# Three page buffers for the sample attention, a seventh expert loaded ahead, and prompt scores in row halves

## What is computed

```
q, k, v, xl, gl = split(x @ w_in)                      # 1024 -> 5 x 512
prompt: s[m] = q[m] k[m]^T / 8, causal, per head, m in (0, 1), 64 wide each
        w = softmax(s[0]) - lam * softmax(s[1]);  o = w v
sample: the same, against 1024 cached keys/values and the 8 new ones
o  = rmsnorm(o) * g;   y = RG-LRU(xl) * gelu(gl)       # recurrence over the tokens
x1 = LN1(alpha * x + [o ; y] @ w_out)                  # 1024 x 1024
group = top-1 of 4, experts = top-2 of the 8 in it     # 32 experts
f  = sum of the two: (silu(x1 wg) * (x1 wu)) wd * weight   # 1024 -> 256 -> 1024
out = LN2(alpha * x1 + f)
```

## Time and profile before

| | |
|---|---|
| time before, median of 3 runs (lowest, highest) | 731.29 us (728.52, 731.52) |
| the profiled execution: its own time | 730.15 us |
| its span, first to last instruction | 728.5 us |
| PE busy | 630.7 us, 87% of the span |
| DVE, ACT, POOL busy | 267.3, 159.0, 111.2 us |
| moved by DMA | 184.46 MB, mean 253 GB/s |
| mean granted TensorE clock (1 is 2.4 GHz) | 0.959 |

### The profile page before, as it was taken

How to read it: one execution, slowest core, us unless ns; L and a number is a source line. 1 busy time by engine, 2 the same in 40 slices (tenths; PEclk the granted TensorE clock), 3 DMA queues, 4 the chain that set the end, 5 groups by cost and what they waited for, 6 DMA issues and landing times.

```text
span 728.5 us, 11355 instructions
## 1 busy us (share of the span) xinstructions
PE 630.7 (87%) x3948; PEld 405.0 (56%) x3948; DVE 267.3 (37%) x566; ACT 159.0 (22%) x322; POOL 111.2 (15%) x191
## 2 busy tenths in 40 slices
PE   6999999999995898979999879899887877777764
PEld 5777676467664565655454636656554444444321
DVE  1562269036456453543544671101110011000257
ACT  2001542143344442431000101111111111111122
POOL 8000000012024133320000002112121111010100
PEclk9999999999998999999999799999999999999987
DMA  9330303153043599972991847999999999999273
GB/s 300 145 113 4 116 0 115 45 184 135 1 141 104 176 363 325 370 278 110 417 385 59 324 187 269 409 416 415 415 419 417 418 418 416 417 415 385 103 287 115
DMA packets 53399, 184.46 MB, mean 253 GB/s; under 512 B 10563, under 2 KB 10563, under 8 KB 44658
## 3 DMA queue, kind: packets, MB, share of 16 engines
q1 hardware_dynamic: 37056, 147.86, 52.1%
q0 software_dynamic: 11328, 29.01, 10.9%
q10 hardware_dynamic: 4978, 7.11, 2.6%
HBM read 174.44 MB, written 18.42 MB: 265 GB/s over the span
## 4 chain that ended last, share of the span: by engine, by line
PE 52%; SPq 20%; DMA 16%; DVE 5%; issue 5%; ACT 3%; POOLq 0%; DVEq 0%; ACTq 0%
PE ps L696 13%; PE ps L930 8%; DMA arena<-in_w_down_e_dram 7%; SPq L384 6%; SPq L387 6%; PE ps L1000 5%; PE ps L745 4%; SPq L383 4%; PE ps L710 4%; DMA arena<-in_cache_k_dram 3%; PE ps L1022 3%; PE ps L816 2%; PE ps L762 2%; DMA arena<-in_w_out_dram 2%; DMA arena<-in_w_in_dram 1%
## 5 line engine op out<-in xcount | busy, mean ns | idle before, releaser
L1000 PE MATMUL ps<-arena 128*64 128x256 f32 x1088 | 124.6, 384 | 14.7 <-DMA arena<-in_w_up_e_dram 13.9
L1000 PEld LDWEIGHTS ps<-arena 128*64 128x64 f32 x1088 | 88.0, 138 | 55.6 <-DMA arena<-in_w_up_e_dram 20.2
L696 PE MATMUL ps<-arena 128*128 128x288 f32 x384 | 95.4, 411 | 1.5 <-DMA arena<-in_w_in_dram 1.4
L1022 PE MATMUL ps<-arena 128*64 128x512 f32 x272 | 68.9, 652 | 25.6 <-DMA arena<-in_w_down_e_dram 15.3
L1722 DVE TENSOR_TENSOR arena<-ps,arena 128x128 f32<-128x128 f32 x34 | 9.9, 292 | 211.7 <-ACT arena L1276 211.7
L696 PEld LDWEIGHTS ps<-arena 128*128 128x128 f32 x384 | 73.7, 193 | 22.5 <-issue 2.0
L1022 PEld LDWEIGHTS ps<-arena 128*64 128x64 f32 x272 | 23.5, 147 | 60.0 <-issue 60.0
L930 PE MATMUL ps<-arena 128*128 128x512 f32 x128 | 56.2, 594 | 0.3 <-DMA arena<-in_w_out_dram 0.3
L816 PE MATMUL ps<-arena 128*128 128x128 f32 x256 | 40.3, 297 | 13.3 <-DVE arena L1502 4.6
L609 POOL DMA_INDIRECT y_rows<-arena x17 | 18.3, 1079 | 180.6 <-ACT arena L1283 153.8
L505 POOL DMA_DIRECT2D arena<-in_cache_v_dram x64 | 34.5, 539 | 69.6 <-PE ps L849 44.4
(11 more groups left out here) (321 smaller groups left out, 768.1 us busy)
## 6 DMA issues: line engine op xcount, KB each, us to landing
arena<-in_w_gate_e_dram SPq DMA_DIRECT2D x34, 1024.0 KB, 17.0
arena<-in_w_up_e_dram SPq DMA_DIRECT2D x34, 1024.0 KB, 24.0
arena<-in_w_down_e_dram SPq DMA_DIRECT2D x34, 1024.0 KB, 24.7
arena<-in_cache_k_dram SPq DMA_DIRECT2D x64, 256.0 KB, 5.4
arena<-in_cache_v_dram POOLq DMA_DIRECT2D x64, 256.0 KB, 6.7
arena<-in_w_in_dram SPq DMA_DIRECT2D x4, 2048.0 KB, 8.5
arena<-in_w_out_dram SPq DMA_DIRECT2D x1, 4096.0 KB, 13.0
x_rows<-arena ACTq DMA_DIRECT2D x8, 512.0 KB, 6.2
```

The source lines that it names most:

```text
L696: last = mm(ps[:, b + h, 0:HALF], win[n % 2][:, k, m * P:(m + 1) * P], xT[:, k, h * HALF:(h + 1) * HALF], start=k == 0, stop=k == KD - 1)
L1000: last = mm(ps[fh * 64:fh * 64 + 64, u, 0:256], xTm[:, k, u * CAP:(u + 1) * CAP], gu[:, :, k, fh * P:(fh + 1) * P], start=k == 0, stop=k = ...
L1022: last = mm(ps[u * 64:u * 64 + 64, 5 + dh, :], hT[u][:, fh * CAP:(fh + 1) * CAP], dn[u][:, fh, dh * W:(dh + 1) * W], start=fh == 0, stop=f ...
```

## The change

Five things are done:

1. **Three buffers each for keys and values.** A buffer is no longer one stretch of SBUF but a list of eight places (`pages`), some in space that earlier stages have left. The waits move by one sequence: the keys of b wait for the transposes of b-3, the values for the products of b-3. The third value buffer lies in the prompt's keys and values, so it waits for the end of the prompt attention, for the state outputs and for DVE's copy of the new keys (`tails_free`). `w_out` is loaded in two halves, the first when sequence 5 is transposed, the second when sequence 6 is.
2. **Elements written out.** The loops over sequences on PE, SP and POOL, SP's loop over the first rounds of expert loads, and PE's round 1 of the experts become straight code. ACT and DVE keep their loops.
3. **A seventh expert ahead.** When the rows are stored and transposed, SP loads expert 6 into the place of `x` and `lng` (`A_SPARE`). The ring then skips a load: slot 0's first tile gets expert 12 where it would have got 6, and in round 1 only its neighbour is reloaded.
4. `x` (rows from `x1_rows`), and LN2's gain and bias, are loaded behind the last expert weights by SP. ACT no longer loads the two.
5. **Prompt scores in row halves.** `qs` has map 0 in rows 0 to 63 and map 1 in rows 64 to 127, and the two maps of a head are multiplied one behind the other, each over its 64 rows. POOL's zeroing of `qz` (4096 elements) goes. One gate half moves: one stands ahead of `scores(2)`, and rounds 0 to 6 have one each; `ends_rows` goes to round 7.

The diff, cut to its core, by engine. The places:

```diff
-        qz = area(A_QZ, NH, 2, SEQ)
+        qs = area(A_QZ, NH, SEQ)
+        A_SPARE = A_X
...
-        kpages = [area(A_WIN + (1 - i) * NPG * W, NPG, W) for i in range(2)]
-        vpages = [area(A_V1, NPG, W), area(A_V, NPG, W)]
+        kpages = [pages((A_WIN + NPG * W, 8)), pages((A_QZ + NH * SEQ, 4), (A_V1 + NPG * W, 3), (A_BD + W, 1)), pages((A_WIN, 8))]
+        vpages = [pages((A_V1, 8)), pages((A_V, 8)), pages((A_KN, 4), (A_VN, 4))]
```

SP's key pages and `w_out`:

```diff
-            keys(0, 0, lambda: sp.wait_ge(s_pj, 25))
-            keys(1, 1, lambda: sp.wait_ge(s_pj, 33))
-            with sp.Fori(1, NB // 2) as jb:
...
-                        sp.wait_ge(s_ktp[1], 4 * b - 4)
...
-            sp.wait_ge(s_ktp[1], 4 * NB)
-            sp.dma_start(wout[:, :, :], A["w_out"][0].rearrange("(k p) n -> p k n", p=P)).then_inc(s_wo, 16)
+                if b == 0:
+                    sp.wait_ge(s_pj, 25)
+                elif b == 1:
+                    sp.wait_ge(s_ends, 1)
+                elif b == 2:
+                    sp.wait_ge(s_pj, 33)
+                else:
+                    sp.wait_ge(s_ktp[1], 4 * (b - 2))
...
+            sp.wait_ge(s_ktp[1], 4 * (NB - 2))
+            sp.dma_start(wout[:, 0:KD // 2, :], wo[:, 0:KD // 2, :]).then_inc(s_wo, 16)
+            sp.wait_ge(s_ktp[1], 4 * (NB - 1))
+            sp.dma_start(wout[:, KD // 2:, :], wo[:, KD // 2:, :]).then_inc(s_wo, 16)
```

SP's expert weights:

```diff
+            sp.wait_ge(s_x1d, 32 * NT)
+            sp.wait_ge(s_x1t, 2 * NT)
+            load_gate_up(2 * RING, A_SPARE, s_wsp)
+            load_down(2 * RING, A_SPARE + GUW, s_wsp)
...
-            with sp.Fori(0, ROUND0 - 2) as prev:
+            for prev in range(ROUND0 - 2):
                 for slot in range(RING):
-                    next_pair(prev, slot, lambda u: 2 * RING * (prev + 1) + 2 * slot + u)
+                    if (prev, slot) == (0, 0):
+                        sp.wait_ge(s_gu[0], 1)
+                        sp.sem_inc(s_wgu[0][0], 32)
+                        next_pair(0, 0, lambda u: (4 * RING, 2 * RING + 1)[u])
+                        sp.sem_inc(s_wd[0][0], 16)
+                    elif (prev, slot) == (1, 0):
+                        next_pair(1, 0, lambda u: 4 * RING + u, parts=(1,))
+                    else:
+                        next_pair(prev, slot, lambda u: 2 * RING * (prev + 1) + 2 * slot + u)
```

SP, behind the last expert weights:

```diff
+            sp.dma_start(x[:, 0:NT - 1, :], x1_dram[0:SEQ].rearrange("(t p) d -> p t d", p=P)).then_inc(s_ln2, 16)
+            sp.dma_start(x[0:TS, NT - 1, :], x1_dram[SEQ:T]).then_inc(s_ln2, 16)
+            sp.dma_start(lng, A["ln2_g"][0:1, :].to_broadcast([P, D])).then_inc(s_ln2, 16)
+            sp.dma_start(lnb, A["ln2_b"][0:1, :].to_broadcast([P, D])).then_inc(s_ln2, 16)
```

POOL's value pages:

```diff
-            pool_link(g.memset(qz, 0.0))
...
+            values(2, tails_free)
             query(1)
-            with q.Fori(1, NB // 2) as jb:
...
-                        q.wait_ge(s_pvs, b - 1)
...
+            for b in range(3, NB):
+                values(b, lambda: q.wait_ge(s_pvs, b - 2))
+                query(b - 1)
+            query(NB - 1)
```

PE, prompt attention:

```diff
-                for m in range(2):
-                    for j, h in enumerate(heads):
-                        last = mm(ps[:, 2 * (n % 2) + m, j * w:(j + 1) * w], qz[:, h, m, i * P:(i + 1) * P], kTn[:, h, 0:w], start=True, stop=True)
+                for j, h in enumerate(heads):
+                    for m in range(2):
+                        half = slice(64 * m, 64 * m + 64)
+                        last = mm(ps[:, 2 * (n % 2) + m, j * w:(j + 1) * w], qs[half, h, i * P:(i + 1) * P], kTn[half, h, 0:w], start=True, stop=True)
...
-            gate_half(1)
...
-                if n < 6:
-                    gate_half(n + 2)
-                if n == 6:
+                if n < 7:
+                    gate_half(n + 1)
+                if n == 7:
                     ends_rows()
```

PE, sequences and experts:

```diff
-            with pe.Fori(0, NB // 2 - 1) as jb:
-                sample(2 * jb + 1, 1)
-                sample(2 * jb + 2, 0)
+            for b in range(1, NB - 1):
+                sample(b, b % 2)
...
-            for slot in range(RING):
-                pair(0, slot)
+            for r in range(2):
+                for slot in range(RING):
+                    pair(r, slot)
...
-            with pe.Fori(1, full) as r:
+            with pe.Fori(2, full) as r:
```

ACT, behind the row stores:

```diff
-            act.dma_start(lng, A["ln2_g"][0:1, :].to_broadcast([P, D])).then_inc(s_ln2, 16)
-            act.dma_start(lnb, A["ln2_b"][0:1, :].to_broadcast([P, D])).then_inc(s_ln2, 16)
```

DVE, ahead of the last sums:

```diff
-            dve.wait_ge(s_x1d, 32 * NT)
-            dve.wait_ge(s_ln2, 32)
+            dve.wait_ge(s_ln2, 64)
```

More of the change, by code:

```diff
@@ L158, in build, with pages @@
         assert A_TMP + 8 * SEQ <= A_V1 and A_V1 + NPG * W <= A_VN and A_LRU + 20 * T <= A_VN
-        kpages = [area(A_WIN + (1 - i) * NPG * W, NPG, W) for i in range(2)]
-        vpages = [area(A_V1, NPG, W), area(A_V, NPG, W)]
+        def pages(*parts):
+            return [area(at + g * W, W) for at, n in parts for g in range(n)]
+        kpages = [pages((A_WIN + NPG * W, 8)), pages((A_QZ + NH * SEQ, 4), (A_V1 + NPG * W, 3), (A_BD + W, 1)), pages((A_WIN, 8))]
+        vpages = [pages((A_V1, 8)), pages((A_V, 8)), pages((A_KN, 4), (A_VN, 4))]
+        assert A_V1 + (NPG + 3) * W <= A_VN and 4 * W <= NH * T and A_QZ + NH * SEQ + 4 * W <= A_X
         kT = area(A_KT, NH, 1152)
@@ L265, in build @@
         s_rs = sem("rms_out"); s_on = sem("o_normed"); s_ot = sem("o_transposed"); s_oe = sem("o_in_cat")
-        s_kin = [sem(f"keys_in{i}") for i in range(2)]; s_vin = [sem(f"values_in{i}") for i in range(2)]
+        s_kin = [sem(f"keys_in{i}") for i in range(3)]; s_vin = [sem(f"values_in{i}") for i in range(3)]
         s_ktp = [sem(f"keys_transposed{i}") for i in range(2)]
@@ L401, in _, with next_pair @@
                     load_down(2 * slot + u, at + GUW, s_wd[slot][u])
-            def next_pair(prev, slot, expert):
+            sp.wait_ge(s_x1d, 32 * NT)
+            sp.wait_ge(s_x1t, 2 * NT)
+            load_gate_up(2 * RING, A_SPARE, s_wsp)
+            load_down(2 * RING, A_SPARE + GUW, s_wsp)
+            def next_pair(prev, slot, expert, parts=(0, 1)):
                 experts = [expert(u) for u in range(2)]
-                for u in range(2):
+                for u in parts:
                     sp.wait_ge(s_gu[u], RING * prev + slot + 1)
@@ L992, in pair @@
                 pe.wait_ge(s_xd, j + 1)
+                spare = isinstance(j, int) and j == RING
+                at = [A_SPARE if spare and u == 0 else (2 * slot + u) * TILEW for u in range(2)]
                 for u in range(2):
-                    pe.wait_ge(s_wgu[slot][u], 32 * r + 32)
-                    gu = area((2 * slot + u) * TILEW, 2, KD, FE)
+                    if spare and u == 0:
+                        pe.wait_ge(s_wsp, 48)
+                    else:
+                        pe.wait_ge(s_wgu[slot][u], 32 * r + 32)
+                    gu = area(at[u], 2, KD, FE)
                     pe.wait_ge(s_info, 1)
@@ L1012, in pair @@
                     pe.wait_ge(s_hc[u], j + 1)
-                    pe.wait_ge(s_wd[slot][u], 16 * r + 16)
-                dn = [area((2 * slot + u) * TILEW + GUW, 2, D) for u in range(2)]
+                    if not (spare and u == 0):
+                        pe.wait_ge(s_wd[slot][u], 16 * r + 16)
+                dn = [area(at[u] + GUW, 2, D) for u in range(2)]
                 if not (isinstance(j, int) and j == 0):
```

58 lines of the change are left out of this document (27 added, 31 removed).

## The result

The changed kernel takes 722.54 us (median of 5; 719.35 to 724.61) beside 731.21 us for the kernel before (728.52 to 731.52): a ratio of 0.989, 95% interval 0.9865 to 0.9915, so 6 to 10 us faster. The forecast was 718.6 us. The profiled execution has 721.78 us, a span of 720.1 us and a mean clock of 0.966.

What follows compares the result with a forecast made beforehand. Bounds by stage: DMA slightly too slow for PE in sample attention, weight loads in the experts' second half, the DVE and ACT chain in prompt attention. 730.15 - 3.7 - 0.35 - 7.7 + 0.3 + 0.4 - 0.5 = 718.6 us; range 714.5 to 724.

Steps and rivals of the forecast that it cites:

- One of the prediction's own signs of being wrong: Experts: a last pair that starts later than 665 us would show the prediction wrong.
- Page buffers, -3.7, and the wait for `w_out`, -0.35: Sample attention: third buffers remove PE's stall for key pages, 3.7 us, and its wait for w_out, 0.35 us.
- so the stall goes whole: Sample attention: a lead over one 11.1 us period outlasts a 1.4 us deficit, so 14.82 - 11.10 = 3.7 us is won.
- Written out, 0: Straight code on PE, SP and POOL: periods with and without a branch are both 11.1 us, so 0.
- The slow rival: Whole program: about six more instruction loads, 5 us or more each if they wait, +30 us, 749 us; 5%.
- Seventh expert, -7.7: Experts: one expert's weights loaded ahead, 3.15 MB, 7.56 us at 416 GB/s, taken as -7.7 us.
- The pace by the spacing of the pairs, 8.3: Experts: an expert is worth half of a pair's spacing, 8.3 us; the forecast would be 718.0.
- The load's cover, +0.3, and the reload, +0.4: Expert load overlaps the first gather, 0 to +2.2, taken +0.3; reload overlaps the scatter, 0 to +2.4, taken +0.4 us.
- The rival by which the seventh expert buys nothing: End: the reload delays the y_rows loads, up to 8.2 us paid for 7.7 won, 726.5 us; 8%.
- Prompt scores, -0.5: Prompt attention: row halves side by side and the moved gate half give -0.5 us, ends -3 and +1.5.
- in series: Prompt scores: the row halves run one after the other, +0.8 instead of -0.5, 719.9 us; 17%.
- the rival that PE is the bound: Prompt attention: half scores count in full, 0.4 to 0.9 us in each of ten steps, 711 to 715 us; 7%.

Runs made afterwards that it cites:

- the run with the earlier scaling: Kernel before with DVE's scaling of x moved ahead of the expert loop, nothing else; 727.87 us in one timed execution.
- the run with filler: Changed kernel with ten products that nobody reads, five ahead of scores(2) and five ahead of transposes(0); 721.07 us in one timed execution.
- the run with the shift alone: Kernel before with only the gate halves one round later; 730.94 us beside 730.03, ratio 1.0015.

## Why the prediction was right or wrong

**The direction and the range were right, the size was 4 us too hopeful.** The median lies in the wide range (714.5 to 724), but 2 us above the 717 to 720.5 that had 63%, and it comes that near because two misses offset each other in part: the prompt attention is 4.1 us worse than its term, the end 1.9 us better. One of the prediction's own signs of being wrong came: the last pair starts at 666.64 us, later than 665. By the sum it would stand near 662; the 4.1 us of the prompt attention are most of the difference. Term by term:

*Page buffers, -3.7, and the wait for `w_out`, -0.35.* The profile shows -3.8, but the term was mis-sized all the same. Four traces with two buffers show 94.35, 91.38, 91.30 and 91.75 us, eight with three show 90.55 to 91.81 (mean 90.9). Against the three ordinary ones (mean 91.5) the third buffer is worth 0.5 us at most: the two groups overlap, and from the first to the eighth sample scores two buffers take 78.6 to 79.2 us in these three, three buffers 78.9 to 79.0 in all eight. What differs lies behind the eighth scores (11.6 to 12.9 us), where PE waits 2.81 us for ACT in every run and the clock behind it differs. The step that failed is "so the stall goes whole": the stall was priced from one execution, and the steady deficit that the same paragraph works out (0.2 us a sequence, 1.4 us in all) was the nearer estimate. Not all of its 3.7 us was a wait, either: behind the 2.91 us the clock is low (0.57 from 280 to 284), and eight products take 1.91 us that take 1.09 elsewhere:

```profile
281.15 1.91 PE L838 MATMUL ps<-arena 128*128 128x128 f32 x8
```

*Written out, 0.* Not quite. With the loop and no wait for keys a sequence takes 11.1 us (276.44 to 287.53), in straight code 11.2 (278.24 to 289.43), with two buffers too: some 0.7 us over the stage. Why, no run here shows. The slow rival is out: the page counts 27 instruction loads where the earlier trace rows has 21, six more as it was estimated, and no engine's wait is put down to them.

*Seventh expert, -7.7.* Right. The eight traces with it take 240.2 to 241.0 us, the four without 247.8 to 248.5: 7.6 us on the means. The pace by the spacing of the pairs, 8.3, would be nearer to the one pair of profiled executions (8.1), and further from the rest.

*The load's cover, +0.3, and the reload, +0.4.* Both nothing. Merge and routing take 0.1 us less (the first gather 4.26 us, where it took 4.36), and DVE's wait for the reload ends 5.8 us ahead of the first sum (692.45 - 686.62). What was not seen: the reload pushes the scaling of `x` out of the scatter's way, and the end takes 1.5 us less here, 2.1 us on the means of the traces (41.8 in eight against 43.9 in three, the run with the earlier scaling left out); about half of that is the scatter, as the experiment shows. The rival by which the seventh expert buys nothing is out.

*Prompt scores, -0.5.* This step failed too, and it is the one that made the forecast too hopeful; it measured +3.6. The halves do run side by side, so the rival "in series" is out: 1.88 us became 1.13. (The Trainium skill's page "TensorEngine Tiling (Array Packing)", section "Theoretical Speedup", has up to 2x; this is 1.66x, and the time it promises by itself, 711, needed PE to be the bound.) "Shorter scores only lengthen the wait" was right too. What failed is that the longer wait was priced at its own length. In the old order it is, and the halves gain 2.2 us (71.82 to 69.66; the rival that PE is the bound wanted 4 to 8). In the new order the waits let the clock fall, and the work behind them runs at half speed: 4.5 of the 5.8 us between the two orders. For the 3.0 us near the start the run with filler ties it to the waits; the 1.5 us at the end came with the same wait in four runs and not in a fifth. The other 1.3 us is left to the order itself. Also, "the moved half gives about 4 us ahead of `scores(2)`" holds with full-height scores alone: in the run with the shift alone step 9 starts 52.8 us after the first scores, against 56.4 in the kernel before, 3.6 us sooner; with row halves the two orders differ by 0.1 us (55.04 and 54.96).

*The base.* PE's first product with `w_in` stands at 14.21 us in the profiled execution of before, at 14.5 to 17.4 in the others, 16.65 and 16.73 with the text of before and an edit elsewhere. So the +1.4 us in the first line of the table can't be laid to the change. The forecast was made against an execution that was lucky there and unlucky in the sample attention.

On the means of the traces the change is worth -0.5 (sample attention, with the writing out in it) +3.6 (prompt) -7.6 (experts) -2.1 (end) = -6.6 us, at the near end of what the medians give (6 to 10). Whether stalls like that of the earlier trace rows are common enough in the kernel before to make up the rest, no run here shows.

## What to carry to other kernels

When an edit takes work from an engine that then waits, ask what the wait does to TensorE's clock: the work behind the wait can lose as much as the wait itself. Filler work that nobody reads kept the clock up in both places where it was tried; it gained 1.1 us in one, and in the other what it gained was lost again by the end of the next stage. So it is to be judged at a point well behind it. Two edits that are harmless alone must be priced together. A stall that stands once in one profiled execution is a sample: look for the steady deficit behind it before it goes into a sum whole.

## What was not expected of the hardware

- Behind PE's two waits of 1.47 and 1.45 us the next gate half took 5.90 us instead of 4.15, at a granted clock of 0.50; with 5.3 us of useless products in place of the waits it took 4.15.
- Behind a wait of 3.48 to 3.50 us at the same place the clock fell in four runs and stayed up in a fifth; behind one of 2.04 us it stayed up in four and fell in one, all with the gate halves in the order of before.
- POOL's scatter of 1.00 us took 2.14 us beside a DVE scaling of 1.22 us, and the loads behind it came 1.1 us later.
- Two products over 64 rows each, one in either row half, take 1.13 us for 512 columns, where the same two over 128 rows took 1.88: 1.66 times faster, with f32.
